# Decayed queries of gated linear attention: from GpSimd to VectorE, with the decays in two PSUM banks

## The chip, the cores and the metric

The kernel runs as one program on one core of a Trainium2 chip. The metric is the device time of one execution in microseconds (us), as the median of several. Within a core, TensorE (PE) multiplies matrices, VectorE (DVE), ScalarE (ACT) and GpSimd (POOL) work on tiles of 128 partitions, and SyncE (SP) issues transfers. Each takes its own instructions in order; they wait for each other by semaphores. TensorE's results go to the eight banks of PSUM, 512 float32 values per partition each; GpSimd works on SBUF alone.

## The reference

A diffusion transformer of four layers over 256 context tokens and 256 latent tokens of width 1024. Each layer has a mixer and a gated feed-forward part with a convolution; layers 0 and 3 mix by window attention, layer 1 by a gated delta net, and layer 2 by gated linear attention, which this change concerns. For each of its 4 heads (key size 128, value size 256) and each of two directions it computes, with `bi` the running sums of the log decays within a chunk:

```python
rel = jnp.exp(jnp.where(tri, bi[:, :, :, None, :] - bi[:, :, None, :, :], -jnp.inf))
a = jnp.einsum('bhid,bhjd,bhijd->bhij', qi, ki, rel)
o = (qi * jnp.exp(bi)) @ s + a @ vi
s = jnp.exp(bl)[:, :, 0, :, None] * s + jnp.einsum('bhjd,bhje->bhde', ki * jnp.exp(bl - bi), vi)
```

The queries decayed from the start of the chunk, `qi * jnp.exp(bi)`, are the quantity whose making the change moves.

## The kernel before

The kernel takes chunks of 128 tokens (four tiles, two of context and two of latents). The layer first projects queries `cq`, keys `ck`, values `cvt`, gates and log decays `cla`, then scans the heads, one after another, both directions in one tile of 2 x 512 values.

Each head has ten steps (`C_STEPS`). TensorE forms the running sums of both directions in banks 2 and 3 (`cumulate`, L1444; for the next head it does so ahead of step 8, after VectorE has read the last of the present ones). ScalarE copies the sums to `cb` (L1015) and takes exponentials into one of three factor buffers `cF`. GpSimd multiplies queries and keys by a factor (`cqf`, `ckf`, L726 and L727), and TensorE turns or multiplies the products.

- Step 0: ScalarE makes the start decays straight from the banks (L1020), GpSimd the decayed queries `cqe` of both directions (L719, L720), TensorE the diagonal product of `ck` and `cq` (L1492).
- Steps 1 and 2: VectorE subtracts each sum from the sum at its tile's end (L2534, into `cX`), ScalarE takes the exponential (L1027), GpSimd multiplies keys by it, TensorE transposes them (L1494) and ScalarE copies them to `ckl` (L1041). They feed the states.
- Steps 3 to 9: one level each, for blocks of 64, 32, 16, 8, 4, 2 and 1 tokens. VectorE subtracts a reference sum (L2539), ScalarE takes four exponentials (L1031, L1033), GpSimd makes two products, TensorE multiplies them (L1496) and VectorE, three steps later, copies the masked result into `cAT` (L2519).

So a head has nine factors: the start decays, the end decays and seven levels. Beside the steps run the six state matmuls of a head (L1455, from its step 5 into step 0 of the next), all into bank 6, each waiting for VectorE's update of the state before it (L2499, L2502), and its four outputs (L1468 and L1470, in steps 2 to 5 of the next head), which use banks 4 and 5 alternately and which ScalarE copies out in steps 6 to 9 (L1007). `cS` holds the states, `cel` the decays of whole tiles (L1018).

The order on every engine is written out by the loop over steps `N`. In one turn of that loop VectorE does: the masked copy of the product of step N-3, the exponents of step N, and the state update of step N-3. ScalarE does: the output copy of step N-4, the exponentials of step N, the copy of turned keys of step N-3. Before the change VectorE's end exponents of a head wait for `f_ready` of the start decays, the semaphore that also tells that the copy before them on ScalarE is made.

Of the kernel before, what the change touches and what calls it, by code (L numbers as in the profile page):

```python
# [19 lines left out]
ALU = mybir.AluOpType  # L20
ACT = mybir.ActivationFunctionType
# [5 lines left out]
P = 128  # L27
# [4 lines left out]
TOK = CTX + SEQ  # L32
TT = TOK // P
# [33 lines left out]
LEVELS = (1, 2, 4, 8, 16, 32, 64)  # L67
# [115 lines left out]
def build(nc, a, out):  # L183
    with ExitStack() as ctx:
# [103 lines left out]
        C_STEPS = NL + 3  # L288
        C_FACTORS = NL + 2
        C_STAGES = C_HEADS * C_STEPS  # L290
# [4 lines left out]
        scan_tile = lambda d, st: st if d == 0 else st ^ 1  # L295
        factor_of = lambda h, step: C_FACTORS * h + (step if step < 2 else step - 1)
        masked_before = lambda N: N // C_STEPS * (C_STEPS - 2) + max(0, N % C_STEPS - 3) + (N % C_STEPS > 0)
# [18 lines left out]
        cX = [sb(f"cX{i}", [P, 2, TOK], at=WH0 + 2 * i * K4) for i in range(2)]  # L316
        cb = sb("cb", [P, 2 * (TOK + 8)], at=LN0 + 3 * K4)
        clow = sb("clow", [33, TOK], at=LN0)
# [118 lines left out]
        la_ready = sem("log_decay_ready")  # L437
        cum_ready = sem("cumulated_ready")
        dx_ready = sem("exponents_ready")
        f_ready = sem("factors_ready")  # L440
# [3 lines left out]
        lv_used = sem("level_product_read")  # L444
        kl_ready = sem("turned_keys_copied")
        x_fin = sem("x_final")
        x_out = sem("x_out_copied")
# [189 lines left out]
        def _(eng):  # L637
# [72 lines left out]
            def linear_attention():  # L710
                for h in range(C_HEADS):
                    for f in range(C_FACTORS):
                        M = h * C_FACTORS + f
                        F = cF[M % 3]
                        eng.wait_ge(f_ready, M + 1)
                        if f == 0:
                            if h >= 2:
                                eng.wait_ge(od_ready, C_OD + TT * (h - 1))
                            eng.tensor_tensor(cqe[:, 0, h % 2, :], cq[:, h, :], F[:, 0], ALU.mult).then_inc(qf_ready, 1)  # L719
                            eng.tensor_tensor(cqe[:, 1, h % 2, :], cq[:, h, :], F[:, 1], ALU.mult).then_inc(kf_ready, 1)  # L720
                            continue
                        before, of = divmod(M - 3, C_FACTORS)
                        if M >= 3 and of > 0:
                            eng.wait_ge(lv_ready, before * C_STEPS + of + 2)
                        src = ck if f == 1 else cq
                        eng.tensor_tensor(cqf[:, M % 3, :], src[:, h, :], F[:, 0], ALU.mult).then_inc(qf_ready, 1)  # L726
                        eng.tensor_tensor(ckf[:, M % 3, :], ck[:, h, :], F[:, 1], ALU.mult).then_inc(kf_ready, 1)  # L727

            def normalised(l):
# [49 lines left out]
        def _(eng):  # L779
# [183 lines left out]
            def linear_attention():  # L963
# [35 lines left out]

                both = banks[:, 2:4, :]  # L1000
                for N in range(C_STAGES + C_STEPS + 4):
                    if N - 4 in OUTS:
                        h, i = OUTS[N - 4]
                        e, t = TT * h + i, C_OUT[i]
                        eng.wait_ge(od_ready, C_OD + e + 1)
                        dst = co[:, 2 * h:2 * h + 2, t * P:(t + 1) * P]
                        eng.activation(dst, bank[4 + e % 2][:, 0:2 * P].rearrange("p (z n) -> p z n", z=2), ACT.Copy).then_inc(bo_ready, 1)  # L1007
                    h, step = divmod(N, C_STEPS)
                    if N < C_STAGES and step != 2:
                        M = factor_of(h, step)  # L1010
                        F = cF[M % 3]
                        if step == 0:
                            eng.wait_ge(cum_ready, h + 1)
                            copies = cb[:, 0:2 * (TOK + 7)].rearrange("p (d c) -> p d c", d=2)[:, :, 0:TOK]
                            eng.activation(copies, both, ACT.Copy)  # L1015
                            for d in range(2):
                                end = bank[2 + d].rearrange("p (t n) -> p t n", t=TT)[:, :, (P - 1) * (1 - d)]
                                eng.activation(cel[:, d, h, :], end, ACT.Exp, scale=1.0 / C_TAU)  # L1018
                            factor_free(M)
                            eng.activation(F[:], both, ACT.Exp, scale=1.0 / C_TAU).then_inc(f_ready, 1)  # L1020
                        else:
                            x = (C_FACTORS - 1) * h + M % C_FACTORS - 1
                            X = cX[x % 2]
                            eng.wait_ge(dx_ready, x + 1)
                            factor_free(M)
                            if step == 1:
                                eng.activation(F[:], X[:], ACT.Exp, scale=1.0 / C_TAU).then_inc(f_ready, 1)  # L1027
                            else:
                                part = lambda t, z: t.rearrange("p (n z b) -> p n z b", z=2, b=LEVELS[NL + 2 - step])[:, :, z, :]
                                for z in range(2):  # L1030
                                    eng.activation(part(F[:, 0], z), part(X[:, 1 - z], z), ACT.Exp, scale=1.0 / C_TAU)  # L1031
                                for z in range(2):
                                    ins = eng.activation(part(F[:, 1], z), part(X[:, z], z), ACT.Exp, scale=-1.0 / C_TAU)  # L1033
                                ins.then_inc(f_ready, 1)
# [169 lines left out]
        def _(eng):  # L1204
# [202 lines left out]
            def linear_attention(l):  # L1407
# [50 lines left out]
                def output(h, i):  # L1458
# [16 lines left out]
                for N in range(C_STAGES):  # L1475
                    h, step = divmod(N, C_STEPS)
                    if step == C_STEPS - 2 and h + 1 < C_HEADS:
                        eng.wait_ge(dx_ready, (C_FACTORS - 1) * (h + 1))
                        cumulate(h + 1)
# [525 lines left out]
        def _(eng):  # L2005
# [464 lines left out]
            def linear_attention(l):  # L2470
# [35 lines left out]
                for N in range(C_STAGES + C_STEPS + 4):  # L2506
# [15 lines left out]
                    if N < C_STAGES and step not in (0, 2):  # L2522
                        M = factor_of(h, step)
                        x = (C_FACTORS - 1) * h + M % C_FACTORS - 1
                        X = cX[x % 2]
                        if step == 1:
                            eng.wait_ge(f_ready, C_FACTORS * h + 1)
                        if x >= 2:
                            eng.wait_ge(f_ready, (x - 2) // (C_FACTORS - 1) * C_FACTORS + (x - 2) % (C_FACTORS - 1) + 2)
                        if step == 1:  # L2530
                            tiles = lambda t: t.rearrange("p (t n) -> p t n", t=TT)
                            for d in range(2):
                                end = tiles(cb[:, d * (TOK + 7):d * (TOK + 7) + TOK])[:, :, (P - 1) * (1 - d)].unsqueeze(2)
                                ins = eng.tensor_tensor(tiles(X[:, d]), end.to_broadcast([P, TT, P]), tiles(bank[2 + d]), ALU.subtract)  # L2534
                        else:
                            b = LEVELS[NL + 2 - step]
                            pair = lambda t: t.rearrange("p d (n m) -> p d n m", m=2 * b)
                            ref = cb[:].rearrange("p (d c) -> p d c", d=2)[:, :, 0:TOK].rearrange("p d (n m) -> p d n m", m=2 * b)[:, :, :, b - 1]
# [285 lines left out]
```

## Time and profile before

| | us |
|---|---|
| median of 3 runs | 2649.49 |
| the runs | 2646.41, 2654.41, 2649.49 |
| profiled execution | 2650.06 |
| its span | 2647.9 |
| mean granted TensorE clock in the span | 0.978 of full speed |

The page of the profile gives busy time by engine over the span; the scan of the four heads is about 110 us of it, from 1697 to 1808 us. Views of a window show that part: "windows" gives busy time and granted clock by stretch, "timeline" the instructions in order of time. Two instructions in a row on VectorE, ScalarE or GpSimd overlap a little in these records, so their start-to-start distance is some 0.05 to 0.1 us below the duration.

### The profile page before, as it was taken

How to read it: one execution, taken by the hardware profiler on the slowest of the kernel's cores; microseconds unless marked ns; L12 is line 12 of the kernel's file. 1: busy time of each engine (PE TensorE's matmuls, PEld its weight loads, DVE VectorE, ACT ScalarE, POOL GpSimd, SP SyncE). 2: the span in 40 equal slices, each digit the busy share in tenths (PEclk: the TensorE clock that was granted, in tenths of full speed). 3: DMA queues.
4: the chain of work that ended last, by engine and by line, in shares of the span. 5: the costliest groups of instructions: out<-in, count | busy, mean ns of one | idle time of the engine just before them, and what ended most of it. 6: DMA issues, size and time to landing. Idle time of an engine off the chain costs nothing.

```text
span 2647.9 us, 43653 instructions
## 1 busy us (share of the span) xinstructions
PE 2502.6 (95%) x15985; PEld 2049.3 (77%) x15985; DVE 1164.5 (44%) x2120; ACT 752.8 (28%) x1539; POOL 1586.7 (60%) x1567
## 2 busy tenths in 40 slices
PE   6999999999999799999999999878999999989997
PEld 4767788887688699778888757866788887678997
DVE  2384511223469787542122330364422223575455
ACT  2263311111541444231111123252311101363332
POOL 2545577775557222557777555685577775655664
PEclk8999999999999899999999999899999999999999
DMA  7355332244523000333334442103323344502552
GB/s 249 101 171 173 115 109 98 96 159 159 177 65 96 32 2 2 116 123 99 100 101 157 161 162 90 55 1 110 129 96 99 101 156 168 196 28 96 184 176 100
DMA packets 217162, 305.07 MB, mean 115 GB/s; under 512 B 7331, under 2 KB 155550, under 8 KB 217023
## 3 DMA queue, kind: packets, MB, share of 16 engines
q1 hardware_dynamic: 190095, 249.66, 28.6%
q10 hardware_dynamic: 26928, 53.48, 5.7%
q8 instruction: 97, 1.59, 0.3%
q14 instruction: 42, 0.34, 0.0%
HBM read 302.07 MB, written 1.05 MB: 114 GB/s over the span
## 4 chain that ended last, share of the span: by engine, by line
PE 80%; DVE 11%; ACT 2%; POOL 2%; issue 2%; DMA 1%; SPq 1%; DVEq 0%; POOLq 0%; ACTq 0%; PEldq 0%
PE bank L1226 42%; PE bank L1945 12%; PE bank L1277 3%; PE bank L1241 2%; PE bank L1976 2%; PE bank L1724 2%; PE bank L1261 2%; PE bank L1774 1%; PE bank L1768 1%; PE bank L1356 1%; PE bank L1332 1%; DVE ztmp L2214 1%; DVE ast L2141 1%; POOL cqf L726 1%; PE bank L1246 1%
## 5 line engine op out<-in xcount | busy, mean ns | idle before, releaser
L657 POOL TENSOR_TENSOR w_lo<-w_raw,w_hi 128x512 fp32r<-128x512 f32 x652 | 858.2, 1316 | 93.7 <-POOL w_hi L654 72.0
L654 POOL TENSOR_SCALAR w_hi<-w_raw 128x512 fp32r<-128x512 f32 x652 | 429.0, 658 | 616.2 <-PE bank L1226 387.0
L1226 PE MATMUL bank<-u_lo,w_hi 128*128 128x512 f32 (+1 forms) x2048 | 759.2, 371 | 9.0 <-DVE u_lo L2062 5.9
L1226 PE MATMUL bank<-u_hi,w_hi 128*128 128x512 f32 (+1 forms) x2048 | 752.0, 367 | 0.0
L1226 PE MATMUL bank<-u_hi,w_lo 128*128 128x512 f32 (+1 forms) x2048 | 751.9, 367 | 0.0
L1226 PEld LDWEIGHTS bank<-u_lo,w_hi 128*128 128x128 f32 x2048 | 389.5, 190 | 88.8 <-issue 18.6
L1226 PEld LDWEIGHTS bank<-u_hi,w_hi 128*128 128x128 f32 x2048 | 389.1, 190 | 63.2
L1226 PEld LDWEIGHTS bank<-u_hi,w_lo 128*128 128x128 f32 x2048 | 389.6, 190 | 61.6
L1945 PE MATMUL bank<-gs_lo,w_hi 128*128 128x512 f32 (+1 forms) x576 | 209.2, 363 | 2.2 <-POOL w_lo L657 2.2
L2748 DVE TENSOR_TENSOR gs_lo<-g,gs_hi 128x512 fp32r<-128x512 f32 (+1 forms) x88 | 108.2, 1240 | 230.2 <-ACT gs_hi L1173 230.2
L1945 PE MATMUL bank<-gs_hi,w_lo 128*128 128x512 f32 (+1 forms) x576 | 208.8, 363 | 0.0
L1945 PE MATMUL bank<-gs_hi,w_hi 128*128 128x512 f32 (+1 forms) x576 | 208.8, 363 | 0.0
L2723 DVE SCALAR_TENSOR_TENSOR cv<-bank,vec,cv 128x510 f32<-128x510 f32 (+1 forms) x88 | 59.6, 678 | 325.6 <-ACT cv L1147 325.4
L1147 ACT ACTIVATE cv<-bank,vec 128x512 f32<-128x512 f32 (+1 forms) x88 | 58.9, 720 | 500.3 <-PE bank L1226 462.0
L2740 DVE TENSOR_TENSOR g<-cv,bank 128x512 f32 (+3 forms) x88 | 50.9, 617 | 197.0 <-PE bank L1226 195.7
L1173 ACT ACTIVATE gs_hi<-g 128x512 fp32r (+3 forms) x88 | 49.4, 575 | 306.3 <-PE bank L1945 249.2
L737 POOL TENSOR_SCALAR ap<-ap,ast 128x512 f32<-128x512 f32 (+1 forms) x48 | 76.4, 1593 | 81.2 <-DVE ast L2152 81.2
L1945 PEld LDWEIGHTS bank<-gs_lo,w_hi 128*128 128x128 f32 x576 | 108.7, 189 | 20.7 <-issue 3.8
L1945 PEld LDWEIGHTS bank<-gs_hi,w_lo 128*128 128x128 f32 x576 | 108.7, 189 | 16.8
L1945 PEld LDWEIGHTS bank<-gs_hi,w_hi 128*128 128x128 f32 x576 | 108.7, 189 | 16.7
L2067 DVE SCALAR_TENSOR_TENSOR x<-bank,gat,x 128x256 f32<-128x256 f32 x112 | 48.7, 479 | 140.8 <-PE bank L1226 74.7
L2100 DVE TENSOR_TENSOR w_lo<-w_raw,w_hi 128x512 fp32r<-128x512 f32 x76 | 68.5, 911 | 89.2 <-ACT w_hi L812 75.8
(350 smaller groups left out, 3757.4 us busy)
## 6 DMA issues: line engine op xcount, KB each, us to landing
w_raw<-in_ffn_w_up SPq DMA_DIRECT2D x88, 1024.0 KB, 5.1
w_raw<-in_ffn_w_down SPq DMA_DIRECT2D x44, 1024.0 KB, 4.9
ada_area<-in_ada_w ACTq DMA_DIRECT2D x39, 1024.0 KB, 15.4
ada_w<-in_ada_w SPq DMA_DIRECT2D x28, 1024.0 KB, 5.2
w_raw<-in_gdn_w_in SPq DMA_DIRECT2D x16, 1024.0 KB, 5.8
w_raw<-in_attn_w_qkv SPq DMA_DIRECT2D x12, 1024.0 KB, 7.9
ada_w<-in_ada_w ACTq DMA_DIRECT2D x12, 1024.0 KB, 6.7
w_raw<-in_gla_w_in SPq DMA_DIRECT2D x12, 1024.0 KB, 5.4
```

The lines of the kernel that those rows point to most:

```text
L654: eng.tensor_scalar(w_hi[:, q, :], src, 1.0, 0.0, ALU.mult, ALU.add).then_inc(pool.own, pool.step())
L657: eng.tensor_tensor(w_lo[:, q, :], src, w_hi[:, q, :].bitcast(F32), ALU.subtract).then_inc(w_split, 1)
L737: eng.tensor_scalar(pj, pj, ast[:, 4, j % 4, 0:1], None, ALU.mult).then_inc(p_ready, 1)
L1147: eng.activation(cv[:, m, T], bank[(PAIR_GATE if pair else 0) + m][:, T], ACT.Identity, bias=vec[:, bass.ds(f + CONVB(l), 1)], scale=vec[: ...
L1226: mm = eng.matmul(bank[banks[m]][:, T], w[:, q, c:c + P], v[:, k, T], start=(k == 0 and n == 0), stop=(k == KT - 1 and n == 2))
L1241: eng.matmul(bank[banks[m]][:, T], w[:, slot, c + m * P:c + (m + 1) * P], u_hi[:, k, T], start=(k == 0 and n == 0), stop=False)
L1261: mm = eng.matmul(bank[banks[m]][:, T], w[:, k // 2, c:c + P], v[:, k, T], start=(k == 0 and n == 0), stop=(k == KT - 1 and n == 2))
L1277: mm = eng.matmul(bank[banks[t]][:, 0:256], v[:, k, t * P:(t + 1) * P], w[:, q, c:c + 256], start=(k == 0 and n == 0), stop=(k == KT - 1 a ...
L1945: mm = eng.matmul(bank[b][:, T], w[:, q, j * P:(j + 1) * P], v[:, s, T], start=(start and q < 2 and n == 0), stop=(stop and q >= 2 and n = ...
L2100: eng.tensor_tensor(w_lo[:, q, :], w_raw[:, s, q * PIECE:(q + 1) * PIECE], w_hi[:, q, :].bitcast(F32), ALU.subtract).then_inc(w_fourth, 1)
L2723: eng.scalar_tensor_tensor(v3(cv[:, m, :], 1, 256), v3(bank[gate + m][:], 0, 255), w0, v3(cv[:, m, :], 1, 256), ALU.mult, ALU.add).then_in ...
L2748: eng.tensor_tensor(gs_lo[:, slot, T], gf, gs_hi[:, slot, T].bitcast(F32), ALU.subtract).then_inc(gs_ready, 1)
```

## The change

- The start decays are no longer one of the factors: a head has eight (`C_FACTORS = NL + 1`), and the two products of GpSimd per head are gone.
- There are two buffers `cb` for the copied sums, for even and odd heads; the second lies in the area of the split weights that is idle in the scan.
- ScalarE copies the sums of head h+1 at the end of step 9 of head h (`sums_copied`), behind the last level's exponentials. Right behind the copy it makes the start decays of head h from the copied sums of head h, with both directions in banks 4 and 5 (`start_decays`), once the outputs of head h-1 have been copied out.
- The tile decays `cel` are made from the copied sums, behind the end factor (`tile_decays`).
- VectorE makes `cqe` of head h for both directions in one instruction with 1024 values per partition at step 0 of head h+1, between the masked copy and the state update of that turn. It waits for the decays (`cb_ready`).
- VectorE's end exponents wait for the copy alone. TensorE's outputs wait for `qe_ready`. GpSimd at its end waits for the last decays.

```diff
-        C_FACTORS = NL + 2
+        C_FACTORS = NL + 1
-        factor_of = lambda h, step: C_FACTORS * h + (step if step < 2 else step - 1)
+        factor_of = lambda h, step: C_FACTORS * h + max(step - 2, 0)
+        c_copied = lambda h: max(1, 2 * h)
+        c_started = lambda h: min(2 * h + 3, 2 * C_HEADS)
...
-        cb = sb("cb", [P, 2 * (TOK + 8)], at=LN0 + 3 * K4)
+        cb = [sb(f"cb{i}", [P, 2 * (TOK + 8)], at=o) for i, o in enumerate((LN0 + 3 * K4, WH0 + 4 * K4))]
...
-                        if f == 0:
-                            if h >= 2:
-                                eng.wait_ge(od_ready, C_OD + TT * (h - 1))
-                            eng.tensor_tensor(cqe[:, 0, h % 2, :], cq[:, h, :], F[:, 0], ALU.mult).then_inc(qf_ready, 1)
-                            eng.tensor_tensor(cqe[:, 1, h % 2, :], cq[:, h, :], F[:, 1], ALU.mult).then_inc(kf_ready, 1)
-                            continue
...
+                eng.wait_ge(cb_ready, 2 * C_HEADS)
...
+                def sums_copied(h):
+
+                    eng.wait_ge(cum_ready, h + 1)
+                    eng.activation(c_sums(h), both, ACT.Copy).then_inc(cb_ready, 1)
+
+                def tile_decays(h):
+
+                    eng.wait_ge(cb_ready, c_copied(h))
+                    for d in range(2):
+                        end = c_sums(h)[:, d].rearrange("p (t n) -> p t n", t=TT)[:, :, (P - 1) * (1 - d)]
+                        eng.activation(cel[:, d, h, :], end, ACT.Exp, scale=1.0 / C_TAU)
+
+                def start_decays(h):
+
+                    eng.wait_ge(bo_ready, C_BO + TT * h)
+                    eng.activation(banks[:, 4:6, :], c_sums(h), ACT.Exp, scale=1.0 / C_TAU).then_inc(cb_ready, 1)
...
+                    if N == 0:
+                        sums_copied(0)
+                    elif N < C_STAGES and step not in (0, 2):
...
+                        if step == 1:
+                            eng.activation(F[:], X[:], ACT.Exp, scale=1.0 / C_TAU).then_inc(f_ready, 1)
+                            tile_decays(h)
...
+                        if step == C_STEPS - 1:
+                            if h + 1 < C_HEADS:
+                                sums_copied(h + 1)
+                            start_decays(h)
...
+                    eng.wait_ge(qe_ready, h + 1)
...
                         if step == 1:
-                            eng.wait_ge(f_ready, C_FACTORS * h + 1)
...
+                            eng.wait_ge(cb_ready, c_copied(h))
...
+                    if step == 0 and 1 <= h <= C_HEADS:
+                        h -= 1
+                        eng.wait_ge(cb_ready, c_started(h))
+                        if h >= 2:
+                            eng.wait_ge(od_ready, C_OD + TT * (h - 1))
+                        eng.tensor_tensor(cqe[:, :, h % 2, :], cq[:, h, :].unsqueeze(1).to_broadcast([P, 2, TOK]),
+                                          banks[:, 4:6, :], ALU.mult).then_inc(qe_ready, 1)
                     if N - 3 in STATES:
                         state_update(*STATES[N - 3])
```

## Rows read from the trace of the kernel before

**Rows 1.** The page: busy us, share of the span and instructions of each engine.

```profile
PE 2502.6 (95%) x15985; PEld 2049.3 (77%) x15985; DVE 1164.5 (44%) x2120; ACT 752.8 (28%) x1539; POOL 1586.7 (60%) x1567
```

**Rows 2.** Windows: stretch, length, busy us by engine, granted clock, DMA.

```profile
1698.70:1722.60 23.90, 15.57 (x80) 12.77 (x79) 14.62 (x18) 13.41 (x35) 21.06 (x18) 0.71 0.01 1
1722.60:1748.20 25.60, 20.11 (x143) 18.09 (x142) 17.36 (x23) 14.60 (x39) 22.38 (x19) 0.93 0.00 1
1748.20:1773.10 24.90, 18.95 (x143) 16.63 (x142) 17.30 (x23) 14.59 (x39) 22.27 (x19) 1.00 0.00 1
1773.10:1799.90 26.80, 19.92 (x135) 17.17 (x133) 18.46 (x25) 14.58 (x39) 23.55 (x20) 0.94 0.00 1
```

**Rows 3.** Timeline of GpSimd, turn to head 2: start, us, instruction, [idle before <-releaser].

```profile
1748.14 1.27 POOL L727 TENSOR_TENSOR ckf<-ck,cF 128x512 f32<-128x512 f32 x1
1750.42 1.26 POOL L719 TENSOR_TENSOR cqe<-cq,cF 128x512 f32<-128x512 f32 x1 [1.00 <-ACT cF L1020]
...
1752.87 1.28 POOL L726 TENSOR_TENSOR cqf<-ck,cF 128x512 f32<-128x512 f32 x1
...
1757.00 1.27 POOL L726 TENSOR_TENSOR cqf<-cq,cF 128x512 f32<-128x512 f32 x1 [1.62 <-ACT cF L1033]
```

**Rows 4.** Waits in the scan: who for whom, us in total, times, longest.

```profile
POOL cqf L726 <- ACT cF L1033: 6.6, 6, 1.6
```

**Rows 5.** Timeline of TensorE, turn to head 2 and the next sums.

```profile
1746.28 1.95 PE L1444 MATMUL bank<-con,cla 128*128 128x128 f32 x16
...
1752.10 0.70 PE L1455 MATMUL bank<-cvt,ckl 128*128 128x256 f32 x2 [1.42 <-DVE cS L2502]
1752.64 1.05 PE L1492 MATMUL bank<-cq,ck 128*128 128x128 f32 x8
...
1771.17 1.95 PE L1444 MATMUL bank<-con,cla 128*128 128x128 f32 x16
```

**Rows 6.** Timeline of ScalarE, turn to head 2.

```profile
1748.27 1.03 ACT L1015 ACTIVATE cb<-bank 128x1024 f32<-128x1024 f32 x1 [1.43 <-PE bank L1444]
1749.19 0.23 ACT L1018 ACTIVATE cel<-bank 128x4 f32<-128x4 f32 x2
1749.30 1.04 ACT L1020 ACTIVATE cF<-bank 128x1024 f32<-128x1024 f32 x1
1751.69 1.06 ACT L1027 ACTIVATE cF<-cX 128x1024 f32<-128x1024 f32 x1 [1.35 <-DVE cX L2534]
```

**Rows 7.** Timeline of VectorE, turn to head 2.

```profile
1746.49 0.48 DVE L2502 SCALAR_TENSOR_TENSOR cS<-cS,cel,bank 128x256 f32<-128x256 f32 x1
1749.16 0.73 DVE L2519 COPY_PREDICATED cAT<-msk,bank 128x512 f32<-128x512 uint8 x1 [2.20 <-PE bank L1496]
1750.37 1.28 DVE L2534 TENSOR_TENSOR cX<-cb,bank 128x512 f32<-128x512 f32 x2 [0.47 <-ACT cF L1020]
...
1754.34 1.22 DVE L2539 TENSOR_TENSOR cX<-bank,cb 128x1024 f32<-128x1024 f32 x1
1755.47 0.47 DVE L2502 SCALAR_TENSOR_TENSOR cS<-cS,cel,bank 128x256 f32<-128x256 f32 x1
```

**Rows 8.** Timeline, start of head 0, ScalarE, VectorE and GpSimd.

```profile
1698.76 1.02 ACT L1015 ACTIVATE cb<-bank 128x1024 f32<-128x1024 f32 x1 [46.76 <-PE bank L1444]
...
1700.86 1.29 DVE L2534 TENSOR_TENSOR cX<-cb,bank 128x512 f32<-128x512 f32 x2 [2.53 <-ACT cF L1020]
...
1705.82 1.28 POOL L726 TENSOR_TENSOR cqf<-cq,cF 128x512 f32<-128x512 f32 x1
```

**Rows 9.** Timeline of TensorE, level-64 products of heads 1 and 2.

```profile
1734.04 1.99 PE L1496 MATMUL bank<-cqf,ckf 128*128 128x128 f32 x8 [2.60 <-POOL ckf L727]
...
1759.64 1.13 PE L1496 MATMUL bank<-cqf,ckf 128*128 128x128 f32 x8 [2.60 <-POOL ckf L727]
```

**Rows 10.** Timeline, end of head 3, ScalarE and TensorE.

```profile
1796.57 0.75 ACT L1033 ACTIVATE cF<-cX 128x256 f32<-128x256 f32 x2
...
1800.04 1.13 PE L1496 MATMUL bank<-cqf,ckf 128*128 128x128 f32 x8 [0.93 <-POOL ckf L727]
```

More of the change, by code:

```diff
@@ L316, in build @@
         cX = [sb(f"cX{i}", [P, 2, TOK], at=WH0 + 2 * i * K4) for i in range(2)]
-        cb = sb("cb", [P, 2 * (TOK + 8)], at=LN0 + 3 * K4)
+        cb = [sb(f"cb{i}", [P, 2 * (TOK + 8)], at=o) for i, o in enumerate((LN0 + 3 * K4, WH0 + 4 * K4))]
+        c_sums = lambda h: cb[h % 2][:, 0:2 * (TOK + 7)].rearrange("p (d c) -> p d c", d=2)[:, :, 0:TOK]
+        c_refs = lambda h: cb[h % 2][:].rearrange("p (d c) -> p d c", d=2)[:, :, 0:TOK]
         clow = sb("clow", [33, TOK], at=LN0)
@@ L438, in build @@
         cum_ready = sem("cumulated_ready")
+        cb_ready = sem("sums_copied_then_start_decays_ready")
         dx_ready = sem("exponents_ready")
@@ L445, in build @@
         kl_ready = sem("turned_keys_copied")
+        qe_ready = sem("queries_decayed_from_start")
         x_fin = sem("x_final")
@@ L715, in linear_attention @@
                         eng.wait_ge(f_ready, M + 1)
-                        if f == 0:
-                            if h >= 2:
-                                eng.wait_ge(od_ready, C_OD + TT * (h - 1))
-                            eng.tensor_tensor(cqe[:, 0, h % 2, :], cq[:, h, :], F[:, 0], ALU.mult).then_inc(qf_ready, 1)
-                            eng.tensor_tensor(cqe[:, 1, h % 2, :], cq[:, h, :], F[:, 1], ALU.mult).then_inc(kf_ready, 1)
-                            continue
[L722 to L725, printed above, removed]
+                        if M >= 3:
+                            before, of = divmod(M - 3, C_FACTORS)
+                            eng.wait_ge(lv_ready, before * C_STEPS + of + 3)
+                        src = ck if f == 0 else cq
                         eng.tensor_tensor(cqf[:, M % 3, :], src[:, h, :], F[:, 0], ALU.mult).then_inc(qf_ready, 1)
                         eng.tensor_tensor(ckf[:, M % 3, :], ck[:, h, :], F[:, 1], ALU.mult).then_inc(kf_ready, 1)
+                eng.wait_ge(cb_ready, 2 * C_HEADS)
             def normalised(l):
@@ L1008, in linear_attention @@
                     h, step = divmod(N, C_STEPS)
-                    if N < C_STAGES and step != 2:
+                    if N == 0:
+                        sums_copied(0)
+                    elif N < C_STAGES and step not in (0, 2):
                         M = factor_of(h, step)
                         F = cF[M % 3]
[L1012 to L1020, printed above, removed]
-                        else:
[L1022 to L1034, printed above, removed]
@@ new lines, in linear_attention @@
+                        X = cX[M % 2]
+                        eng.wait_ge(dx_ready, M + 1)
+                        factor_free(M)
+                        if step == 1:
+                            eng.activation(F[:], X[:], ACT.Exp, scale=1.0 / C_TAU).then_inc(f_ready, 1)
+                            tile_decays(h)
+                        else:
+                            part = lambda t, z: t.rearrange("p (n z b) -> p n z b", z=2, b=LEVELS[NL + 2 - step])[:, :, z, :]
+                            for z in range(2):
+                                eng.activation(part(F[:, 0], z), part(X[:, 1 - z], z), ACT.Exp, scale=1.0 / C_TAU)
+                            for z in range(2):
+                                ins = eng.activation(part(F[:, 1], z), part(X[:, z], z), ACT.Exp, scale=-1.0 / C_TAU)
+                            ins.then_inc(f_ready, 1)
@@ L1477, in linear_attention @@
                     if step == C_STEPS - 2 and h + 1 < C_HEADS:
-                        eng.wait_ge(dx_ready, (C_FACTORS - 1) * (h + 1))
+                        eng.wait_ge(dx_ready, C_FACTORS * (h + 1))
                         cumulate(h + 1)
@@ L2523, in linear_attention @@
                         M = factor_of(h, step)
-                        x = (C_FACTORS - 1) * h + M % C_FACTORS - 1
-                        X = cX[x % 2]
+                        X = cX[M % 2]
                         if step == 1:
-                            eng.wait_ge(f_ready, C_FACTORS * h + 1)
-                        if x >= 2:
-                            eng.wait_ge(f_ready, (x - 2) // (C_FACTORS - 1) * C_FACTORS + (x - 2) % (C_FACTORS - 1) + 2)
+                            eng.wait_ge(cb_ready, c_copied(h))
+                        if M >= 2:
+                            eng.wait_ge(f_ready, M - 1)
                         if step == 1:
@@ L2532, in linear_attention @@
                             for d in range(2):
-                                end = tiles(cb[:, d * (TOK + 7):d * (TOK + 7) + TOK])[:, :, (P - 1) * (1 - d)].unsqueeze(2)
+                                sums = tiles(c_sums(h)[:, d])
+                                end = sums[:, :, (P - 1) * (1 - d)].unsqueeze(2)
                                 ins = eng.tensor_tensor(tiles(X[:, d]), end.to_broadcast([P, TT, P]), tiles(bank[2 + d]), ALU.subtract)
@@ L2537, in linear_attention @@
                             pair = lambda t: t.rearrange("p d (n m) -> p d n m", m=2 * b)
-                            ref = cb[:].rearrange("p (d c) -> p d c", d=2)[:, :, 0:TOK].rearrange("p d (n m) -> p d n m", m=2 * b)[:, :, :, b - 1]
+                            ref = pair(c_refs(h))[:, :, :, b - 1]
                             ins = eng.tensor_tensor(pair(X[:]), pair(both), ref.unsqueeze(3).to_broadcast([P, 2, TOK // (2 * b), 2 * b]),
```

## The prediction

> **What bounds the kernel now.** The page first: TensorE is busy for 95% of the span and GpSimd for 60% [rows 1], but the change touches one stage only, the scan over the four heads of gated linear attention, so the share over the whole span says little. The view by windows cuts that stage at the ends of the running sums of heads 0, 1, 2 and 3: 23.9, 25.6, 24.9 and 26.8 us [rows 2]. In the middle two GpSimd is busy for 22.4 of 25.6 and 22.3 of 24.9 us, TensorE for some 20, VectorE 17, ScalarE 15. That looks like a GpSimd bound with 2.6 to 3.2 us of idle time per head. The timeline tells where those are. GpSimd ends head 1's last factor at 1749.41, waits 1.00 us for the start decays and, after four products, another 1.62 us for the level-64 factor, which it starts at 1757.00 [rows 3]. Waits of this second kind come to 6.6 us in six waits [rows 4]. So each turn from one head to the next is a latency chain through all engines, and only the stretch from level 64 to the last level runs at GpSimd's pace (two products take 2.45 us, 1750.42 to 1752.87 [rows 3]; seven factors are 17.2 us).
>
> I count the turn from head 1 to head 2 from 1748.23, when TensorE ends the running sums of head 2 (1746.28 + 1.95) [rows 5]. ScalarE copies them at 1748.27, makes the small tile decays at 1749.19 and the start decays at 1749.30 to 1750.34 [rows 6]. VectorE starts the end exponents at 1750.37, because it waits for the start decays too, and goes on to level 64's exponents at 1754.34 [rows 7]. Between these two lie two state updates and TensorE's first product of head 2 (1752.64), itself behind a state matmul that stood still for 1.42 us until VectorE had updated a state [rows 5]. ScalarE turns the end exponents into a factor at 1751.69 [rows 6] and GpSimd multiplies it from 1752.87 [rows 3]. From 1757.00 it is 16.12 us until the next sums end (1771.17 + 1.95 = 1773.12) [rows 3, 5]; 8.77 + 16.12 are the 24.9 us of the window.
>
> **The change part by part.**
>
> *Taken from GpSimd:* two products per head, eight in all, at 1.23 us from start to start (1748.14 + 1.27 = 1749.41 is the end of the last before the gap) [rows 3]: 9.8 us of work. In heads 1 to 3 they lie just in the time in which the end factor is being made, so their going uncovers ScalarE and VectorE, and takes nothing from level 64, which is late by 1.62 us as it is.
>
> *ScalarE's order:* at the end of head h come the copy of head h+1's sums, then the start decays of head h. The 1.4 us of ScalarE's gap ahead of the copy stay empty, as the decays stand behind a copy that waits for those sums. The decays now start where the tile decays stood, 1749.19, and with the 1.04 us of the same activation [rows 6] end at 1750.23. Their output in a PSUM bank is not shown by any row of ScalarE here. The four quarter-size exponentials of one level factor take some 1.43 us for as many elements (two pairs of 0.75 us, of which 1796.57 is the second) [rows 10]; so I bound it by 0.93 and 1.43 us and take 1.04, the row with the same shape. The Trainium skill (ScalarE: Activation LUTs, "Step-by-step: what each stage is for") says PSUM is the quicker destination for an activation, without a figure that fits here; no row here shows it, and by it the sum would be slightly lower. The tile decays go behind the end factor, which ends at 1752.75 [rows 6], and ScalarE's next exponents are ready at 1755.56 [rows 7]: 2.8 us of cover, so nothing; without it they would cost 0.1 us.
>
> *VectorE's new product:* one of 128x1024 with one bank operand, as the level exponents are; those take 1.13 us until the next start (1754.34 to 1755.47) [rows 7]. Bounds are 1.13 and 1.28 us (the pair of end exponents). It is put at step 0 of the next head: behind one masked copy, but ahead of the third state update (1746.49 before), the next masked copy (1749.16) and the end exponents (1750.37) [rows 7]. That is the place that matters: VectorE takes its work in order, and the product waits for the decays until 1750.23, so it starts at 1750.26. Then come the state update (0.48, with 0.09 of overlap 0.39) and the masked copy (0.73, so 0.64), both of which had been done in idle time. The end exponents start at 1750.26 + 1.13 + 0.39 + 0.64 = 1752.42 in place of 1750.37: **2.05 us later**.
>
> *What is late next:* GpSimd gets the end factor at 1754.9 and stands idle for 5.5 us. The chain to level 64 starts from the end exponents as before. The state matmul behind the late update runs 1751.9 to 1752.6, before VectorE needs it at 1753.6, and the last level product follows it to 1753.5, before its masked copy at 1754.0; so nothing is added, and all keeps its distance. Level 64 goes from 1757.00 to 1759.05, and the stretch behind it keeps its 16.12 us, as its factors, buffers and products are the same. Three turns: 3 x 2.05 = 6.15 us.
>
> *Head 0* has no decays to make before it: VectorE starts the end exponents after the copy (1698.76 + 1.02), at 1699.82, not 1700.86 [rows 8]. ScalarE follows 1.32 us behind, GpSimd 1.13 us behind that, at 1702.27, and two products later starts level 64 at 1704.73 in place of 1705.82: 1.09 us gained.
>
> *The end of head 3:* no turn hides the last product. ScalarE ends its last factor at 1797.32 [rows 10]; decays to 1798.3, VectorE's product to 1799.4, update to 1799.9. TensorE's state matmul then runs at 1799.9 (0.6 us), in front of the last level product, which starts at 1800.48 and not at 1800.04 [rows 10]: 0.44 us lost.
>
> *At nothing:* the second sums buffer, the third operand waits, TensorE's wait for the product (done 5 us before the outputs), GpSimd's wait for the last decays (1798.3, before its own end).
>
> Sum: -1.09 + 6.15 + 0.44 = +5.5 us.
>
> *TensorE's clock.* At the end of the 2.6 us in which TensorE stood still ahead of the level-64 product, the granted clock was down in head 1 (that product took 1.99 us) and up in head 2 (1.13 us, after as long a stop) [rows 9]. Head 1's window at a mean clock of 0.93 is 0.7 us longer than head 2's at 1.00 [rows 2]. With two longer stops in every turn I let head 2 fall too: +0.7, so **+6.2 us** in all. The Trainium skill (TensorE: Matmul & The Clock Gate, "HAM oscillation — how this bites in real kernels") has it that stops between bursts cost the clock again and again; the trace agrees with 0.71, 0.93 and 0.94 in three of four windows, and that is a rule against this change.
>
> The profiled execution took 2650.06 us (span 2647.9), 0.6 above the median of 2649.49; 2650.06 + 6.2 = 2656.3, and against the median 2655.7.
>
> **The rivals.**
>
> *The decays cost nothing* (faster side). If VectorE reached the product when the decays were long there, every turn would gain as head 0 does, since the end exponents no longer wait for the decays: 4 x -1.09 = -4.4 us, 2645.1. For it: ScalarE is busy for only 14.6 of 24.9 us [rows 2]. Against: the decays stand behind the copy and the product ahead of the exponents. It decides in each turn at the point where the product could start before the copy is done. 10%.
>
> *GpSimd's work counts in full:* 9.8 us less, 2639.7. For it: GpSimd is busy for 88% of its windows. Against: its 1.62 us of idle time ahead of level 64 with the products still there. 4%.
>
> *The clock falls within the turn.* At 1.2 GHz eight matmuls take 1.99 us, not 1.13 [rows 9]. The first product and one state matmul lie on the turn's chain: 0.9 + 0.4 (estimate, from the same ratio) in three turns is 3.8 on top of 6.2: +10.0, 2659.5. For it: by the times above TensorE now stands still for over 2 us just after the sums, and then again. Against: in the turns of before the clock held. 13%.
>
> *The forecast,* +6.2: 70%, its own range 2652 to 2660 (costs from +4.6 with the lower bounds and no further fall of the clock, to +8, and the scatter of three runs between 2646.41 and 2654.41). Unnamed: 3%.
>
> **How the numbers follow.** The likeliest case gives 2655.7. The range 2649 to 2662 leaves out the GpSimd case, most of the free case and the upper end of the clock case. About 0.3% (7.9 us, 2641.5 to 2657.4) is what can be told from no change. The forecast lies inside it but near the upper edge: three quarters of its 70% fall within, a quarter above; of the clock case most is above; the free case is mostly within. Faster 5%, same 65%, slower 30%.
>
> **What would show it.** Right: GpSimd idle for about 5.5 us before the end factor of heads 1 to 3, with ScalarE's end factor as releaser; VectorE's new product starting 2.0 us after the sums are done, the end exponents 4.2 us after (2.1 before); windows from sums to sums of 22.8, 27.7 and 27.6 us; the last output copy some 6 us later. Wrong: a turn in which the product starts before the copy ends, an idle time of GpSimd under 3.5 us, ScalarE's exponential into the banks far from 1.04 us, or a change of time outside the scan.

## The result: 0.25% slower, by three longer turns between heads

The changed kernel took 2655.7 us in the median of 20 runs, the kernel before 2649.2: the ratio is 1.0025 (95% interval 1.0017 to 1.0033), or +6.6 us (+4.5 to +8.7). 2655.7 was forecast. On the page the span of the profiled execution went from 2647.9 to 2650.6 us only. A single execution can't be read so finely: over the traces kept here the running sums of head 0 begin anywhere from 1693 to 1701 us, and in these two 3.0 us sooner in the changed kernel. Inside the scan, from the end of head 0's running sums to the end of the last output copy, the two traces give 109.3 us before and 116.1 us after: +6.8 us.

The view by windows of the changed kernel, cut at the ends of the sums as in [rows 2] (stretch, length, busy us of PE, PEld, DVE, ACT and POOL, granted clock, DMA share and GB/s):

```profile
1695.60:1718.30 22.70, 15.52 (x81) 12.66 (x80) 14.14 (x17) 12.55 (x34) 18.44 (x15) 0.70 0.01 1
1718.30:1746.90 28.60, 21.49 (x143) 19.70 (x142) 18.35 (x24) 14.65 (x39) 20.10 (x18) 0.88 0.00 1
1746.90:1774.80 27.90, 20.74 (x143) 19.32 (x142) 18.26 (x24) 14.65 (x39) 19.68 (x16) 0.88 0.00 1
1774.80:1803.50 28.70, 19.18 (x134) 16.90 (x133) 20.10 (x27) 15.54 (x40) 21.18 (x19) 0.94 0.00 1
```

GpSimd is busy for 2.3 to 2.6 us less in each stretch, as it was to be, and yet each stretch but the first is longer: 28.6 and 27.9 us in place of 25.6 and 24.9. The turn to head 2 shows why. Its sums end at 1746.91 (1744.96 + 1.95). First ScalarE and VectorE from the timeline (start, us, instruction, [idle before <- releaser]), which answer to [rows 6, 7]:

```profile
1746.95 1.02 ACT L1006 ACTIVATE cb<-bank 128x1024 f32<-128x1024 f32 x1 [1.44 <-PE bank L1459]
1747.87 1.02 ACT L1018 ACTIVATE bank<-cb 128x1024 f32<-128x1024 f32 x1
1752.37 1.06 ACT L1037 ACTIVATE cF<-cX 128x1024 f32<-128x1024 f32 x1 [3.48 <-DVE cX L2550]
```

```profile
1748.92 1.22 DVE L2563 TENSOR_TENSOR cqe<-cq,bank 128x1024 f32<-128x1024 f32 x1 [3.76 <-ACT bank L1018]
1750.06 0.47 DVE L2518 SCALAR_TENSOR_TENSOR cS<-cS,cel,bank 128x256 f32<-128x256 f32 x1
1750.45 0.72 DVE L2535 COPY_PREDICATED cAT<-msk,bank 128x512 f32<-128x512 uint8 x1
1751.07 1.27 DVE L2550 TENSOR_TENSOR cX<-cb,bank 128x512 f32<-128x512 f32 x2
...
1755.55 1.22 DVE L2555 TENSOR_TENSOR cX<-bank,cb 128x1024 f32<-128x1024 f32 x1
```

VectorE stands still for 3.76 us for the decays, then makes the product, the update and the masked copy in one go, and only then the end exponents, at 1751.07: 4.16 us behind the sums, 2.14 before. ScalarE still waits 1.44 us ahead of the copy, with the decays behind it. GpSimd has nothing to do in that time, which answers to [rows 3]:

```profile
1753.50 1.27 POOL L726 TENSOR_TENSOR cqf<-ck,cF 128x512 f32<-128x512 f32 x1 [5.43 <-ACT cF L1037]
...
1758.21 1.27 POOL L726 TENSOR_TENSOR cqf<-cq,cF 128x512 f32<-128x512 f32 x1 [2.21 <-ACT cF L1044]
```

And TensorE, which answers to [rows 5]; the first two of these matmul groups take 1.22 and 1.92 us where 0.70 and 1.05 are usual:

```profile
1750.59 1.22 PE L1470 MATMUL bank<-cvt,ckl 128*128 128x256 f32 x2 [2.78 <-DVE cS L2518]
1751.60 1.92 PE L1512 MATMUL bank<-cqf,ckf 128*128 128x128 f32 x8
1753.31 0.71 PE L1470 MATMUL bank<-cvt,ckl 128*128 128x256 f32 x2
```

The second of them is the last level product of head 1, and VectorE then waits for it ahead of its masked copy:

```profile
1753.55 0.74 DVE L2535 COPY_PREDICATED cAT<-msk,bank 128x512 f32<-128x512 uint8 x1 [0.82 <-PE bank L1512]
```

From the same timelines, for all kernels below: "turn" is the time from the end of a head's sums to GpSimd's start on its level 64, for heads 1, 2, 3; "stretch" goes from there to the next sums in heads 1 and 2, and to the end of GpSimd's last product in head 3; "scan" is the whole, from the end of head 0's sums to the end of the last output copy. Times in us.

| kernel | exponents behind sums | turns | stretches | scan | ratio to before (95%) |
|---|---|---|---|---|---|
| before | 2.14 | 8.8, 8.8, 8.8 | 16.8, 16.1, 18.0 | 109.3 | |
| changed | 4.15 | 11.7, 11.3, 10.8 | 16.8, 16.6, 17.9 | 116.1 | 1.0025 (1.0017 to 1.0033) |
| changed, again | 4.15 | 11.8, 11.3, 10.8 | 16.8, 16.6, 17.9 | 116.1 | 1.0022 (1.0013 to 1.0031) |
| decays first | 1.69 | 8.3, 8.3, 8.3 | 16.8, 16.1, 17.3 | 106.3 | 0.9989 (0.9979 to 0.9999) |
| update first | 3.76 | 11.7, 10.6, 10.8 | 16.8, 16.8, 17.9 | 115.5 | 1.0024 (1.0014 to 1.0033) |
| before, own wait | 1.55 | 8.2, 8.2, 8.2 | 16.8, 16.1, 17.3 | 106.8 | 0.9985 (0.9977 to 0.9994) |
| product behind | 1.55 | 9.3, 9.3, 9.3 | 16.9, 18.0, 19.1 | 112.5 | 1.0009 (1.0001 to 1.0018) |
| changed, filled | 4.16 | 10.8, 10.8, 10.8 | 16.1, 16.1, 17.3 | 113.0 | 1.0003 (0.9994 to 1.0012) |
| all three first | 1.09 | 7.8, 7.8, 7.8 | 16.8, 16.8, 17.9 | 105.8 | 0.9987 (0.9978 to 0.9997) |
| product behind, filled | 1.55 | 9.3, 10.6, 10.1 | 16.1, 16.1, 17.3 | 110.3 | 0.9993 (0.9984 to 1.0003) |
| all first, filled | 1.10 | 7.8, 7.8, 7.8 | 16.1, 16.1, 17.3 | 103.6 | 0.9982 (0.9971 to 0.9993) |
| before, filled | 2.14 | 8.8, 8.8, 8.8 | 16.1, 16.1, 17.3 | 107.6 | 0.9996 (0.9987 to 1.0005) |

### The profile page after: what moved, and what is told of

It is laid out like the page before. It is cut to its first block, busy times and chain, and to the rows that moved or that the text cites. A ratio compares the mean times of both kernels' runs of the same rounds, so it can differ in the third digit from the quotient of the medians.

```text
span 2650.6 us, 43664 instructions
## 1 busy us (share of the span) xinstructions
PE 2500.9 (94%) x15985; PEld 2050.2 (77%) x15985; DVE 1164.7 (44%) x2124; ACT 752.4 (28%) x1539; POOL 1572.3 (59%) x1559
## 3 DMA queue, kind: packets, MB, share of 16 engines
q1 hardware_dynamic: 190095, 249.66, 28.6%
HBM read 302.07 MB, written 1.05 MB: 114 GB/s over the span
## 4 chain that ended last, share of the span: by engine, by line
PE 79%; DVE 11%; POOL 3%; ACT 2%; issue 2%; DMA 1%; SPq 1%; DVEq 0%; POOLq 0%; ACTq 0%; PEldq 0%
PE bank L1241 41%; PE bank L1961 13%; PE bank L1292 3%; PE bank L1256 2%; PE bank L1992 2%; PE bank L1740 2%; PE bank L1276 2%; PE bank L1790 1%; PE bank L1784 1%; POOL cqf L726 1%; PE bank L1371 1%; PE bank L1347 1%; DVE ast L2157 1%; POOL ckf L727 1%; DVE ztmp L2230 1%
## 5 line engine op out<-in xcount | busy, mean ns | idle before, releaser
L1241 PE MATMUL bank<-u_lo,w_hi 128*128 128x512 f32 (+1 forms) x2048 | 758.3, 370 | 10.6 <-DVE u_lo L2078 6.0
L1961 PEld LDWEIGHTS bank<-gs_hi,w_hi 128*128 128x128 f32 x576 | 108.7, 189 | 16.9
L1961 PEld LDWEIGHTS bank<-gs_hi,w_lo 128*128 128x128 f32 x576 | 108.7, 189 | 16.6
```

What stands on the lines that cost most here:

```text
L1241: mm = eng.matmul(bank[banks[m]][:, T], w[:, q, c:c + P], v[:, k, T], start=(k == 0 and n == 0), stop=(k == KT - 1 and n == 2))
L1961: mm = eng.matmul(bank[b][:, T], w[:, q, j * P:(j + 1) * P], v[:, s, T], start=(start and q < 2 and n == 0), stop=(stop and q >= 2 and n = ...
```

## The experiments

### Decays ahead of the copy

```diff
+                            start_decays(h)
                             if h + 1 < C_HEADS:
                                 sums_copied(h + 1)
-                            start_decays(h)
```

(and the counts of `cb_ready` that go with the order)

> The changed kernel with one swap on ScalarE: the start decays of head h stand ahead of the copy of head h+1's sums, in the 1.4 us for which ScalarE waits for these sums. Theory A (VectorE takes its product in order and has to wait there for decays that stand behind a copy): the decays end about 0.5 us before the sums do, the product runs while VectorE would stand idle, and the end exponents start 1.7 us after the sums (4.15 in the changed kernel, 2.1 before). Turns from sums to level 64 on GpSimd: 8.3 to 8.4 us (11.7, 11.3, 10.8 in the changed kernel). Time: 9 us under the changed kernel, 2 to 3 us under the kernel before (ratio about 0.999). Theory B (it is the product's own 1.13 us on VectorE that costs, wherever the decays are made): end exponents 3.2 us after the sums, turns near 10 us, time 3 to 4 us above before.

Measured: ratio 0.9989, the scan 106.3 us, 9.8 us under the changed kernel. VectorE in the turn to head 2 (sums at 1745.07):

```profile
1744.61 1.22 DVE L2563 TENSOR_TENSOR cqe<-cq,bank 128x1024 f32<-128x1024 f32 x1 [1.27 <-ACT bank L1018]
1745.74 0.47 DVE L2518 SCALAR_TENSOR_TENSOR cS<-cS,cel,bank 128x256 f32<-128x256 f32 x1
1746.14 0.72 DVE L2535 COPY_PREDICATED cAT<-msk,bank 128x512 f32<-128x512 uint8 x1
1746.75 1.27 DVE L2550 TENSOR_TENSOR cX<-cb,bank 128x512 f32<-128x512 f32 x2
```

The same four instructions in the same order, but the first starts 0.46 us before the sums are done and not 2.01 us after them. Turns of 8.3 us are theory A to a tenth; at 10 us theory B is out. The product costs nothing where it lies in VectorE's idle time; what cost was that it waited for something behind the sums.

### The state update ahead of the product

```diff
+                    if N - 3 in STATES:
+                        state_update(*STATES[N - 3])
                     if step == 0 and 1 <= h <= C_HEADS:
...
-                    if N - 3 in STATES:
-                        state_update(*STATES[N - 3])
```

> The changed kernel with one swap on VectorE: at step 0 the state update goes ahead of the new product. The wait for the decays stays. Theory A: only the update's 0.39 us leave the chain to the end exponents, which start 3.75 us after the sums; turns 0.4 us shorter each. Beside it TensorE's state matmul runs early again and the stop of 2.8 us behind the last sums becomes two shorter ones, so if that stop is what let the clock fall within turns 1 and 2 (another 0.9 and 0.5 us there), these go too. Time: 5.3 us above before by the update alone, 3.9 us with the clock. Rival (the late state update is what sets the turn, not the wait): turns back to some 9 us and the time within 1 us of before.

Measured: 1.0024, the scan 115.5 us. The exponents start at 3.76 us (0.39 less, as expected), and with turns of 10.6 us and more the rival is out. Level 64 did not get these 0.39 us in every turn: head 1's turn stayed at 11.7 us, head 2's fell by 0.65 us and head 3's stayed at 10.8. The lower clock did not go, and the stop behind the last sums did not get shorter (2.87 and 3.04 us, 2.79 in the changed kernel). In head 3's turn, where the clock had held, it now fell: the first product of the head took 1.47 us, 1.05 at full clock, and VectorE waited 0.83 us for it. Head 2's stretch rose to 16.8 us. The scan is 6.2 us above before, more than the 3.9 us that I expected with the clock and the 5.3 us without; the ratio of whole times (+3.7 to +8.7 us) can't tell these apart.

### The kernel before, with a wait of its own for the copy

```diff
-                            eng.activation(copies, both, ACT.Copy)
-                            for d in range(2):
...
+                            eng.activation(copies, both, ACT.Copy).then_inc(cb_ready, 1)
+                            eng.wait_ge(cb_ready, h + 1)
                             factor_free(M)
-                            eng.activation(F[:], both, ACT.Exp, scale=1.0 / C_TAU).then_inc(f_ready, 1)
+                            eng.activation(F[:], copies, ACT.Exp, scale=1.0 / C_TAU).then_inc(f_ready, 1)
...
-                            eng.wait_ge(f_ready, C_FACTORS * h + 1)
+                            eng.wait_ge(cb_ready, h + 1)
```

> The kernel before, with GpSimd's two products per head kept. ScalarE makes start and tile decays from the copied sums and no longer from the banks, and VectorE's end exponents wait for the copy alone. Theory A (the turn is a chain over the end exponents, GpSimd's two products are covered by it): the exponents start after the masked copy at 1.55 us behind the sums (2.1 before), level 64 comes 0.6 us sooner in each of three turns, head 0 gains nothing since GpSimd's products come first there: 1.5 to 2 us under before, ratio 0.9993. Rival (GpSimd's 18 products per head set the pace): no change within 0.5 us.

Measured: 0.9985, the scan 106.8 us, that is 2.5 us less. Turns fell from 8.77 to 8.17 us, as said; another 0.7 us came in the last stretch (17.3 and not 18.0), where the clock held this time. GpSimd keeps its two products per head here and the gain is there all the same: they lie beside the making of the end factor, and taking them away was worth nothing in these turns. The wait alone, with ScalarE still reading banks 2 and 3 while VectorE does, was not tried. This kernel also says what the move itself is worth once the waits are right: with no work moved the scan is 106.8 us, with the work moved and the decays first it is 106.3. The move gains in head 0 (6.1 us from the sums to level 64, and not 7.2) and nothing in the turns (8.3 and 8.2), and the ratios of whole times, 0.9989 and 0.9985, do not tell the two kernels apart.

### The product behind the end exponents

```diff
-                    if step == 0 and 1 <= h <= C_HEADS:
+                    if step == 1 and 1 <= h <= C_HEADS:
```

> The changed kernel with VectorE's product moved by one step, behind the end exponents of the next head and ahead of the state update there. ScalarE's order as in the changed kernel. Theory A: the exponents start at 1.55 us behind the sums, the product waits for nothing, and only the state updates behind it are late, by 0.5 us against before. GpSimd gets the end factor early (idle about 3 us before it), level 64 at 9.3 us behind the sums. With head 0's gain of 1.1: 0.5 to 1 us above before, 5.5 us under the changed kernel. Theory B (the product's own time): as the changed kernel, 5 to 6.5 us above before.

Measured: 1.0009, the scan 112.5 us: above the expected sum, though the turns are the 9.3 us of theory A. VectorE in the turn to head 2 (sums at 1745.39):

```profile
1746.32 0.73 DVE L2535 COPY_PREDICATED cAT<-msk,bank 128x512 f32<-128x512 uint8 x1 [2.19 <-PE bank L1512]
1746.95 1.27 DVE L2550 TENSOR_TENSOR cX<-cb,bank 128x512 f32<-128x512 f32 x2
1748.13 1.22 DVE L2563 TENSOR_TENSOR cqe<-cq,bank 128x1024 f32<-128x1024 f32 x1
1749.26 0.48 DVE L2518 SCALAR_TENSOR_TENSOR cS<-cS,cel,bank 128x256 f32<-128x256 f32 x1
```

The product waits for nothing, and only the update behind it is late. The excess lies in the stretches of heads 2 and 3, 18.0 and 19.1 us against 16.1 and 17.3. The timeline of TensorE behind the level-64 product of head 2:

```profile
1757.33 2.05 PE L1512 MATMUL bank<-cqf,ckf 128*128 128x128 f32 x8 [3.75 <-POOL ckf L727]
1759.17 0.64 PE L1484 MATMUL bank<-cAT,cvt 128*128 128x128 f32 x2
...
1760.88 1.92 PE L1512 MATMUL bank<-cqf,ckf 128*128 128x128 f32 x8
1762.59 0.63 PE L1484 MATMUL bank<-cAT,cvt 128*128 128x128 f32 x2
```

After a stop of 3.75 us it runs at the lower clock, two level products (2.05 and 1.92 us, 1.13 at full clock) and the outputs between them back to back; for these microseconds TensorE is the bound, and GpSimd's factors wait.

### Keeping TensorE busy in the stops

```diff
+                    if h >= 1 and step == 3:
+                        for _ in range(11):
+                            eng.matmul(bank[(0, 1, 7)[N % 3]][:, 0:P], ident, con[:, 0:P], start=True, stop=True)
...
+                    if step == C_STEPS - 2 and h + 1 < C_HEADS:
+                        eng.wait_ge(lv_used, masked_before(N - 1))
+                        for _ in range(11):
+                            eng.matmul(bank[(0, 1, 7)[(N + 1) % 3]][:, 0:P], ident, con[:, 0:P], start=True, stop=True)
```

> The changed kernel with extra matmuls on TensorE that nobody reads, in the time in which it stands still: 11 of 128 columns behind the last but one level product of heads 0 to 2 (a stop of 2.8 us) and 11 ahead of the level-64 product of heads 1 to 3 (stops of 3.6, 3.2 and 2.7 us), each some 0.22 us. Theory A (of the 6.5 us, about 5.5 are the order of waits and the rest is TensorE at the lower clock in and behind the turns): turns from sums to level 64 all at 10.8 us (11.7, 11.3, 10.8 in the changed kernel), level 64 to the next sums 16.1 us in heads 1 and 2 (16.8 and 16.6), the scan from 116.1 to about 113 us, time 3 us under the changed kernel and 3.5 us above before (ratio 1.0013). Rival (the clock costs nothing, the stops are in the shadow of other waits): no change against the changed kernel, ratio 1.0025. If the extra matmuls themselves hold something up: above the changed kernel.

Measured: turns 10.8, 10.8, 10.8 and stretches 16.1, 16.1, 17.3, the scan 113.0 us, all as theory A has it. TensorE in the turn to head 2, with the matmuls that nobody reads on L1520 (11 matmuls, 22 records):

```profile
1746.81 2.62 PE L1520 MATMUL bank<-con 128*128 128x128 f32 x22
1749.76 0.70 PE L1470 MATMUL bank<-cvt,ckl 128*128 128x256 f32 x2 [0.33 <-DVE cS L2525]
1750.30 1.05 PE L1515 MATMUL bank<-cqf,ckf 128*128 128x128 f32 x8
```

and the window of that head (26.9 us where the changed kernel had 27.9):

```profile
1746.10:1773.00 26.90, 23.89 (x186) 21.70 (x186) 18.30 (x24) 14.65 (x39) 19.82 (x17) 1.00 0.00 1
```

The granted clock stays at 1.00 and the groups are back at 0.70 and 1.05 us. So 3.0 us of the scan were the lower clock in and behind the turns (in head 0 it is down for 14 us with and without the filling); the 10.8 us turns that are left are the order of the waits by itself. The ratio of whole times, 1.0003 (at most 1.0012, or +3.2 us), lies below what the scan says (+3.8 us); where that rest is, these traces do not show.

Filling with 14 matmuls, ahead of the level-64 product alone, in the kernel with the product behind the exponents (the wait that stood ahead of the second group is kept in this kernel and in "all first, filled", with no matmuls behind it):

> The kernel with the product behind the end exponents, with 14 matmuls that nobody reads ahead of the level-64 product of heads 1 to 3, where TensorE stood still for 3.8 us and then ran the outputs of the head before at the lower clock. There the stretch from level 64 to the next sums was 16.9 and 18.0 us and the last one 19.1, against 16.1 and 17.3 at the full clock. Theory A (this is the clock): 16.1, 16.1 and 17.3 us, turns 9.3 as they are, the scan from 112.5 to 108.1 us, 1 us under before (ratio 0.9996). Rival (something else in that order, VectorE or the banks): no change, ratio 1.001.

Measured: the stretches are 16.1, 16.1 and 17.3 us, so their excess was the clock. But the turns of heads 2 and 3 grew to 10.6 and 10.1, and the scan is 110.3 us, not 108.1. With only this stop filled the clock now fell in the stop just behind the sums, as TensorE shows in the turn to head 2:

```profile
1754.45 1.22 PE L1470 MATMUL bank<-cvt,ckl 128*128 128x256 f32 x2 [1.95 <-DVE cS L2525]
1755.46 1.91 PE L1511 MATMUL bank<-cq,ck 128*128 128x128 f32 x8
```

And in the kernel before, filled with 10 in the same place:

> The kernel before, with 10 matmuls that nobody reads ahead of the level-64 product of heads 1 to 3 and nothing else. It tells how much of the gain of the last kernel is the clock, which the kernel before could have as well. Theory A: level 64 to the next sums 16.1 us in head 1 too (16.8), the last stretch 17.3 us (18.0), turns as they were at 8.8: the scan from 109.3 to 107.9 us, 1.4 us under before, ratio 0.9995. Rival (clock without effect in this order): ratio 1.000 and 109.3 us.

Measured: 107.6 us in the scan (1.7 less), ratio 0.9996 (0.9987 to 1.0005), too small to tell from the whole time. The filling is worth 1.7 us without any other change.

### All three orders

Decays ahead of the copy, the state update ahead of the product, and at step 1 the exponents and the update ahead of the masked copy:

```diff
+                    if N % C_STEPS == 1 and N < C_STAGES:
+                        exponents(N)
+                        if N - 3 in STATES:
+                            state_update(*STATES[N - 3])
+                        masked_copy(N)
+                    else:
+                        masked_copy(N)
+                        exponents(N)
```

> The changed kernel in the order that the first runs point to. ScalarE: decays ahead of the copy. VectorE: at step 0 the state update ahead of the product; at step 1 the end exponents and the state update ahead of the masked copy. By the chain: end exponents at 1.15 us behind the sums (2.14 before, 4.15 changed), level 64 at 7.7 to 7.8 us (8.77 before) in three turns, head 0 gains 1.1 us as in the changed kernel: 4.2 us under before, ratio 0.9984, the scan 105 us. Rival (with the exponents this early another chain, over TensorE's state matmuls and first product, sets level 64): turns stay at 8.3 us as in the kernel with the decays first, time 2.9 us under before.

Measured: exponents at 1.09 us, turns of 7.8 us in all three heads, so no other chain sets level 64. The sum fell short by 0.8 us (105.8, not 105.0): in this order all three stretches had the fall of the clock (16.8, 16.8, 17.9). Filled with 10 matmuls:

> The kernel with decays, update and exponents first, and 10 matmuls that nobody reads ahead of the level-64 product of heads 1 to 3. By theory A one or two falls of the clock behind the turns go (0.7 us each): 0.7 to 1.4 us under the same kernel without them, 5 us under before (ratio 0.998). Rival (the clock costs nothing here): equal to it.

```profile
1721.40:1745.30 23.90, 21.23 (x163) 18.98 (x162) 18.29 (x25) 14.65 (x39) 19.99 (x18) 1.00 0.00 1
1745.30:1769.30 24.00, 21.32 (x163) 19.07 (x162) 18.39 (x25) 14.66 (x39) 19.89 (x17) 1.00 0.00 1
```

103.6 us, 5.7 less than before and 12.5 less than the changed kernel; the ratio is 0.9982 (0.9971 to 0.9993), 4.8 us under before. This is the lowest ratio of all kernels here, and it lies under both the kernel before and the changed one, though VectorE still makes the decayed queries from decays in the banks. Its interval overlaps those of the kernel before with its own wait and of "decays first"; only the scan (103.6 against 106.8 and 106.3 us) sets it apart. The two windows that were 25.6 and 24.9 us are 23.9 and 24.0.

### The changed kernel again

> The changed kernel once more as it is, beside these runs. Theory A: end exponents 4.15 us behind the sums in every turn again, as a fixed chain; level 64 at 10.8 us where the clock holds and up to 0.9 us later where it falls, not necessarily in the same turns as before; time 5.5 to 7 us above before (ratio 1.0021 to 1.0026). Rival (the first comparison was chance): a ratio within 0.0005 of 1.

Measured: 1.0022 and 116.1 us; the first turn took 11.75 us and the others 11.31 and 10.77, to 0.02 us as in the first trace. I had thought that the falls of the clock might move about; they come at the same places again, in the two executions that were profiled.

## Why the prediction was right, point by point

- **The bound.** Each turn is a chain through all engines and GpSimd's work is covered there. Shown by the kernel before with a wait of its own: GpSimd's eight products kept, 2.5 us gained; and by the changed kernel, where they are gone and time is lost.
- **The decays.** In the turn to head 2, forecast to start 0.96 us behind the sums' end and to take 1.04 us; 0.96 and 1.02. The unknown cost, the output in a bank, was small.
- **The product** 1.13 us, start at 2.03 us behind the sums; 1.14 and 2.01 in all three turns. **End exponents** 2.05 us later in each turn; 4.15 against 2.14 is 2.01.
- **What is late next.** Level 64 in head 3's turn, where the clock held, is 2.01 us later, and with the stops filled so it is in all three. GpSimd's idle time ahead of the end factor was put at 5.5 us; 5.27, 5.43, 5.25.
- **Head 0.** Forecast -1.09; level 64 came 1.10 sooner (6.06 against 7.16 us behind the sums), and the window is 1.25 us shorter.
- **The end of head 3.** 0.44 us was too much. The last level product does start late by 0.23 us, but the way from GpSimd's end to the last output copy grew from 8.04 to 8.19 us only.
- **TensorE's clock** was put too low, and partly in the wrong place. I forecast 0.7 us, in head 2's stretch. There it cost 0.5 us (16.6 against 16.1), and another 0.95 and 0.5 us within the turns of heads 1 and 2, which was the third rival's place, at 1.5 of its 3.8 us. In head 1's turn the way was the rival's: a state matmul took 1.22 us and the first product 1.53, and VectorE waited 0.48 and 0.84 us for them. In head 2's it was the last level product, which I had ending 0.5 us before VectorE needs it: it took 1.92 us, and VectorE waited 0.82 us for it. Against it stands that head 0 and the last stretch were 0.1 to 0.2 us better. The kernels with filled stops give the sizes: the lower clock cost the changed kernel 3.0 us and the kernel before 1.7 us, so the change added 1.4 us by it, twice the forecast. Without it, filled against filled, the scan is 5.4 us longer (113.0 and 107.6), where the sum ahead of the clock term was 5.5.
- **The sum** by stretches: -1.25 (head 0), +2.97, +3.01, and +2.07 from head 3's sums to the end are 6.80 us in the scan, where +6.2 was forecast. The windows from sums to sums were forecast at 22.8, 27.7 and 27.6 us and took 22.7, 28.6 and 27.9. That the median came out at 2655.7 to the tenth is luck: the scan alone is 0.6 us off, and the interval of the whole difference is 4 us wide.

The rival "the decays cost nothing" describes the kernel with the decays ahead of the copy, not this one: the point from which it decides, a product that starts before the copy, is met there by 0.5 us and its time is under before. "GpSimd's work counts in full" was shown wrong by the kernel before with a wait of its own and by "decays first": the first keeps GpSimd's products, the second does without them, and their turns are 8.2 and 8.3 us.

## What to carry to other kernels

Before moving work to an engine that has idle time, find where in its queue the work will stand, what it waits for there, and what is queued behind it; an engine that works in order hands its wait on to everything behind. Put into a gap only what is ready when the gap begins: the decays fitted into ScalarE's 1.4 us ahead of the copy, and behind it the scan was 9.8 us longer. And read an engine's share of busy time by stretch: here GpSimd was busy for 88% of its windows and yet taking a ninth of its work away gained nothing in the turns.

## What the runs showed of the hardware

- ScalarE's exponential of 1024 values per partition took 1.02 us from SBUF into two banks and 1.06 us from SBUF to SBUF (both above). This agrees with the Trainium skill (ScalarE: Activation LUTs, "Step-by-step: what each stage is for"), which calls PSUM the quicker destination; here that is 0.04 us.
- In this scan TensorE's granted clock goes from 2.4 to 1.2 GHz at stops of some 2 to 4 us among short bursts, and comes back after some microseconds of work: eight short matmuls take 1.9 to 2.05 us in place of 1.05 to 1.13. The stop that brings it down is not always the longest one: in head 3's turn of the changed kernel it held through one of 2.79 us and fell at one of 2.66. Filling one stop can move the fall to another ("product behind, filled", at 1.95 us). Together the falls in and behind the turns cost the changed kernel 3.0 us of 116. The Trainium skill (TensorE: Matmul & The Clock Gate, "HAM oscillation — how this bites in real kernels") has a loop in which the stop between bursts brings the clock down in every pass; here it comes again and again too, but not at every stop: in the kernel before it fell in head 1 and held in head 2, after 2.60 us each.
